# Order of ScalarE's weight parts in the seven-product MLPs, and where the conditioning slabs of block three are loaded

## The reference, cut to what matters

```
def squared_relu_mlp(h, w_in, w_out):                 # width 4096, twice, in block one
    return jnp.square(jax.nn.relu(h @ w_in)) @ w_out
def swiglu(h, w_gate, w_up, w_down):                  # width 2816, twice, in block two
    return (jax.nn.silu(h @ w_gate) * (h @ w_up)) @ w_down
def swiglu_ffn(h, w_ffn_in, w_ffn_out):               # width 2816, once, in block three
    gate, up = jnp.split(h @ w_ffn_in, 2, axis=-1)
    return (jax.nn.silu(gate) * up) @ w_ffn_out
mod = jax.nn.silu(c) @ w_ada + b_ada                  # c: 1024 values, w_ada: 1024 x 6144
```

## Time and profile before

| | |
|---|---|
| median of 3 runs | 3456.21 us (3449.58 to 3465.32) |
| the profiled execution's own time | 3448.42 us |
| its span, first to last instruction | 3446.5 us |
| mean granted TensorE clock | 0.992 |
| busy: PE, PEld | 3295.1 us (96%), 2701.5 us (78%) |
| busy: DVE, POOL, ACT | 2036.9 us (59%), 1803.1 us (52%), 1105.2 us (32%) |
| read from HBM | 308.15 MB |
| chain that ended last | PE 76%, DVE 11%, POOL 5%, ACT 4%, DMA 2% |

### The profile page before, as it was taken

How to read it: one execution, slowest core, us unless ns; L and a number is a source line. 1 busy time by engine, 2 the same in 40 slices (tenths; PEclk the granted TensorE clock), 3 DMA queues, 4 the chain that set the end, 5 groups by cost and what they waited for, 6 DMA issues and landing times.

```text
span 3446.5 us, 51330 instructions
## 1 busy us (share of the span) xinstructions
PE 3295.1 (96%) x21318; PEld 2701.5 (78%) x21318; DVE 2036.9 (59%) x3132; ACT 1105.2 (32%) x2317; POOL 1803.1 (52%) x1387
## 2 busy tenths in 40 slices
PE   8999999999978989999999988999999999999998
PEld 6768788986767778888878778778887776778996
DVE  6554444458476567688662475564436657657665
ACT  2241101357443344344402432110002225224443
POOL 7526566641234457455666001666665735745563
PEclk9999999999999999999999999999999999999999
DMA  5203434320123333233333101423323635513231
GB/s 178 77 29 106 134 100 145 100 68 26 38 86 110 110 110 116 86 113 109 116 98 110 38 2 43 143 92 98 97 87 126 221 92 176 171 44 104 93 114 52
DMA packets 262152, 341.08 MB, mean 99 GB/s; under 512 B 10016, under 2 KB 202784, under 8 KB 259360
## 3 DMA queue, kind: packets, MB, share of 16 engines
q1 hardware_dynamic: 239408, 301.51, 27.3%
q10 hardware_dynamic: 22512, 36.28, 3.0%
HBM read 308.15 MB, written 25.43 MB: 97 GB/s over the span
## 4 chain that ended last, share of the span: by engine, by line
PE 76%; DVE 11%; POOL 5%; ACT 4%; DMA 2%; issue 1%; ACTq 0%; DVEq 0%; SPq 0%; POOLq 0%
PE bank L130 74%; POOL wlo L153 3%; DVE wlo L153 2%; PE bank L133 2%; ACT whi L148 1%; DVE hl L153 1%; DVE scr L153 1%; POOL sq L153 1%; DMA raw<-in_ffn_w_gate 1%; ACT gt L148 1%; POOL whi L160 1%; DVE macc L163 0%; DVE st L168 0%; DMA raw<-in_w_mlp_in 0%; ACT ah L148 0%
## 5 line engine op out<-in xcount | busy, mean ns | idle before, releaser
L153 POOL TENSOR_TENSOR wlo<-raw,whi 128x512 fp32r<-128x512 f32 x762 | 1060.5, 1422 | 474.0 <-ACT whi L148 460.9
L130 PE MATMUL bank<-ah,whi 128*128 128x512 f32 (+1 forms) x2408 | 869.3, 361 | 33.7 <-ACT scr L148 9.3
L160 POOL TENSOR_SCALAR whi<-raw 128x1024 fp32r<-128x1024 f32 x313 | 364.2, 1182 | 1015.9 <-PE bank L130 506.7
L130 PE MATMUL bank<-ah,wlo 128*128 128x512 f32 (+1 forms) x2408 | 859.9, 357 | 0.0
L130 PE MATMUL bank<-al,whi 128*128 128x512 f32 (+1 forms) x2408 | 848.3, 357 | 0.9 <-DVE al L163 0.9
L130 PEld LDWEIGHTS bank<-ah,whi 128*128 128x128 f32 x2408 | 452.8, 188 | 125.2 <-ACT scr L148 10.1
L130 PEld LDWEIGHTS bank<-al,whi 128*128 128x128 f32 x2408 | 452.8, 188 | 77.2 <-DVE al L163 1.8
L130 PEld LDWEIGHTS bank<-ah,wlo 128*128 128x128 f32 x2408 | 453.1, 188 | 73.5 <-issue 0.2
L130 PE MATMUL bank<-hh,whi 128*128 128x512 f32 x1040 | 417.2, 401 | 23.4 <-DVE hl L153 23.4
L130 PE MATMUL bank<-hl,whi 128*128 128x512 f32 x1040 | 414.0, 398 | 0.0
L130 PE MATMUL bank<-hh,wlo 128*128 128x512 f32 x1040 | 413.1, 397 | 0.0
(11 more groups left out here) (484 smaller groups left out, 5394.2 us busy)
## 6 DMA issues: line engine op xcount, KB each, us to landing
raw<-in_w_in SPq DMA_DIRECT2D x34, 1024.0 KB, 5.3
raw<-in_w_mlp_in SPq DMA_DIRECT2D x32, 1024.0 KB, 5.5
raw<-in_w_mlp_out SPq DMA_DIRECT2D x32, 1024.0 KB, 5.2
raw<-in_w_ada SPq DMA_DIRECT2D x24, 1024.0 KB, 5.2
raw<-in_ffn_w_gate SPq DMA_DIRECT2D x22, 1024.0 KB, 5.5
raw<-in_ffn_w_up SPq DMA_DIRECT2D x22, 1024.0 KB, 5.3
raw<-in_w_ffn_in SPq DMA_DIRECT2D x22, 1024.0 KB, 5.1
raw<-in_w_out SPq DMA_DIRECT2D x16, 1024.0 KB, 5.2
```

What stands on the lines that cost most here:

```text
L130: return self.eng.matmul(out, lhsT, rhs, start=start, stop=stop, skip_group_check=True)
L153: return IDLE if self.eng is None else self.eng.tensor_tensor(out, a, b, op)
L160: return self.eng.tensor_scalar(out, a, s1, s2, op0, op1)
```

## The change

It does two things. In each step of a seven-product MLP ScalarE makes the high parts of the down tiles before it copies P1, not after. And the number of conditioning calls becomes a count that each MLP is given: mlp0 makes one call behind each `first(g)` and two behind each `second(g-1)` (8 + 14 = 22 calls), mlp1 one in each step as before (14, calls 22 to 35), and ffn1 none. The calls in mlp0 take 15 slabs and 7 sets of matmuls (10 and 5 before), those in mlp1 take 9 slabs and 5 sets (10 and 4 before).

```diff
@@ mlp_pe
             if g:
                 second(g - 1)
-                if ada and g < len(groups):
+                for _ in range(ada if g < len(groups) else 0):
                     self.ada_pe(e)
@@ paired_act
+            self.outs_high_act(a, o)
             some(parts, 1)
-            self.outs_high_act(a, o)
             some(high, not opens)
@@ mlp_dve
-                if ada and not end:
+                for _ in range(0 if end else ada):
                     self.ada_dve(d)
@@ relu_mlp_pe
-        self.mlp_pe(e, name, None, (self.A["w_mlp_in"][l], 0), self.A["w_mlp_out"][l], 32, self.mlp1_t[l], True,
+        self.mlp_pe(e, name, None, (self.A["w_mlp_in"][l], 0), self.A["w_mlp_out"][l], 32, self.mlp1_t[l], 2 - l,
@@ relu_mlp_dve
-        self.mlp_dve(d, name, False, 32, self.mlp1_t[l], add, True, True, True, nxt, amid=amid)
+        self.mlp_dve(d, name, False, 32, self.mlp1_t[l], add, True, True, 2 - l, nxt, amid=amid)
@@ ffn2_pe
-                    22, self.mlp1_t[0], name == "ffn1", self.roots_once(e, f"n{name}", prev, False),
+                    22, self.mlp1_t[0], 0, self.roots_once(e, f"n{name}", prev, False),
@@ ffn2_dve
-        self.mlp_dve(d, name, True, 22, self.mlp1_t[0], add, True, name == "ffn1", name == "ffn1", nxt,
+        self.mlp_dve(d, name, True, 22, self.mlp1_t[0], add, True, name == "ffn1", 0, nxt,
@@ ffn3_pe and ffn3_dve: False becomes 0
```

More of the change, by code:

```diff
@@ L4086, in ffn3_pe @@
         W = self.A["w_ffn_in_3"][0]
-        self.mlp_pe(e, "ffn3", (W, 0), (W, 2816), self.A["w_ffn_out_3"][0], 22, self.mlp1_t[0], False,
+        self.mlp_pe(e, "ffn3", (W, 0), (W, 2816), self.A["w_ffn_out_3"][0], 22, self.mlp1_t[0], 0,
                     opening=lambda parts: self.opening_pe(e, self.ln1, parts), last=self.ln2)
@@ L4100, in ffn3_dve @@
         add = lambda d, n, bank, out: d.stt(out, bank[:, :], self.mod(5, n), self.x[:, n, :], MUL, ADD)
-        self.mlp_dve(d, "ffn3", True, 22, self.mlp1_t[0], add, False, False, False, None)
+        self.mlp_dve(d, "ffn3", True, 22, self.mlp1_t[0], add, False, False, 0, None)
         self.ln2_dve(d)
```

## The result

The changed kernel takes 3403.99 us (median of 4 runs, 3400.13 to 3407.53), beside 3454.68 us for the kernel before (4 runs, 3449.58 to 3465.32). The ratio is 0.9849, with a 95% interval of 0.9823 to 0.9875: 50.7 us faster, about 1.5%. The forecast was 3398. The profiled execution took 3404.76 us; the sum for it was 3393, so in the terms 11.8 us are missing; most of them can be found one by one.

What follows compares the result with a forecast made beforehand. TensorE, busy 3295.1 of 3446.5 us, bounds the kernel, so only its holes can be gained. Terms -31.6 - 7.1 - 7.1 - 20.7 + 11 = -55.5 us give 3393, adjusted to 3398 us; 8-in-10 range 3378 to 3428.

Steps and rivals of the forecast that it cites:

- -33.4 in twelve steps: mlp1: of 37.0 us of stalls in twelve steps, 3.6 stay once the down tiles' high parts come first.
- The stalls left: mlp1: 0.3 us of stall remains in each step, bounds 0 and 1.2.
- The fifth call of the third kind: mlp1: one more conditioning call of the sort costing TensorE 1.79 us, with narrow matmuls and a wait for x: +1.8 us.
- The landing that was foreseen as the next late thing: mlp1: the next pair's slab lands 5.0 us into the step; its loop of 20.8 us just fits TensorE's 21.0.
- -7.1 each for the order: ffn1 and ffn3: high parts first save 3.6 us in fifteen steps and 3.5 in the four-out step, each.
- the wide step's 4.1: ffn3's first step with four outs takes 25.14 us, 4.1 over its matmuls; 3.5 of that was to go.
- the missing conditioning: ffn1: without conditioning slabs, pair slabs no longer land late and its rotation becomes ffn3's: -20.7 us, bounds -10 and -22.
- the mis-sized term: mlp0: five more slabs and two more matmul sets cost +11 us, from queued loads and waits; bounds +2 and +35.
- Rival 1: mlp1: VectorE, slowed beside GpSimd, becomes the bound at 23.4 us a step; only 15.6 of 33.4 come: 3416 us, chance 0.16.
- Rival 2: mlp0 pays at every half group because GpSimd never gets ahead: +35 in place of +11, 3422 us, chance 0.12.
- Rival 3: No change: the landing alone sets P5 in mlp1, and mlp0 takes what ffn1 gives: about 3450 us, chance 0.07.
- Rival 4: Slower: the down slab has not landed when ScalarE asks for it, so P1 is late: 3530 us, chance 0.05.

Runs made afterwards that it cites:

- Experiment 2: The changed kernel with ScalarE's old order, so the moved conditioning calls alone: 3457.54 us, ratio 1.0008 to the kernel before.
- experiment 1: The kernel before with only ScalarE's down-tile high parts put ahead of P1, conditioning calls unmoved: 3403.55 us, ratio 0.9859.
- experiment 3: The changed kernel with mlp0's conditioning slab load placed between the next half group's two weight slabs, not ahead of both: 3386.6 us.
- experiment 5: The 3386.6 us kernel (experiment 3) with mlp1's macc ahead of the hidden low parts and mods behind the next step's additions: 3375.15 us.
- experiment 4: The kernel before with the down tiles' high parts moved still later, behind P5: 3598.8 us, ratio 1.0421.

## Why the prediction was right, and where its sizes were off

**The total.** 3398 stands nearer to 3403.99 than the terms deserve, by luck. The terms were 11.8 us short for the profiled execution. The 4.9 us added at the end, mostly for the median standing 7.8 over that execution, hid part of this; in the changed kernel the median stands 0.8 under the profiled execution.

**mlp1.** Forecast -33.4 in twelve steps, measured 296.24 - 264.04 = -32.2. The stalls left were taken as 0.3 us a step; they are (264.04 - 252.0 - 7.2) / 12 = 0.4. The fifth call of the third kind: forecast +1.8, the end of mlp1 measured +2.0. The signs came as named: steps of 21.1 to 22.1 (forecast 21.3) and 22.8 (forecast 23) us, waits for ScalarE's `gt` of 0 (under 5). The landing that was foreseen as the next late thing does hold P5 up in the step shown, where the high part waits 1.31 us for it and P5 is done at 6.6 and not at 5.2; but it is in time, and only four of the twelve steps have such a wait (5.1 us in all).

**ffn3 and ffn1.** Forecast -7.1 each for the order. ffn3: -3.4 and -4.1, together -7.5, though 1.4 were lost between ffn3's start and these steps. Of the wide step's 4.1 I had left 0.6 standing; it went down to the matmuls. Part of it had been clock: 0.93 in the earlier trace rows, 1.00 after. In ffn1 the order and the missing conditioning together gave 24.1 and 4.2 us, forecast 27.8. Experiment 2 has the conditioning at 20.0 (forecast 20.7), so the term was right in size. That the holes were the loads is in part argued: experiment 2 takes away the loads and VectorE's conditioning work at once (its busy time falls from 198.83 to 174.13 us). What speaks for the loads are ScalarE's waits for a landing just ahead of such holes (4.41 us in the earlier trace rows, 6.24 in experiment 1), and that VectorE is busier than before in the changed kernel's ffn1 (206.23 us) while TensorE has no hole there.

**mlp0, the mis-sized term.** Forecast +11, measured +17.7 in it and +1.1 up to mlp1. The waits were forecast well: 8 us, a larger one at every second group border; the trace has 8.9 in four (2.4, 2.3, 2.1 and 2.1, at every second border) and 0.8 in one, less the 0.6 of before, and two sets make 1.6. The other 7.0 us are in no wait. Most of them are in the matmuls behind each wait:

```profile
424.70 0.47 PE L130 MATMUL bank<-ah,whi 128*128 128x512 f32 x1 [2.26 <-POOL wlo L153]
...
425.95 0.63 PE L130 MATMUL bank<-al,whi 128*128 128x512 f32 x1
426.38 0.63 PE L130 MATMUL bank<-ah,wlo 128*128 128x512 f32 x1
...
428.89 0.39 PE L130 MATMUL bank<-ah,wlo 128*128 128x512 f32 x1
429.12 0.40 PE L130 MATMUL bank<-ah,whi 128*128 128x512 f32 x1
```

Their pitch is 0.43 us, not 0.233, for about 3.5 us. The sums of that stretch, and of the one behind the first late group's wait:

```profile
424.70:428.94 4.24, 4.24 (x12) 3.34 (x13) 3.23 (x3) 0.00 (x0) 4.16 (x3) 0.60 0.02 4
...
329.24:333.20 3.96, 3.96 (x11) 3.10 (x12) 3.22 (x3) 0.00 (x0) 3.88 (x3) 0.58 0.02 4
```

Granted clock 0.60 and 0.58: most of it at the 1.2 GHz level, after TensorE had done nothing but narrow matmuls and waiting for 3.2 and 3.4 us. Twelve matmuls at 0.233 would take 2.8 us and took 4.24. Over the first forty matmuls behind each of the four waits it is 10.96 us against 9.42 for the same ones in experiment 3, which has no wait there: each wait costs 1.5 us more than its row in the list of waits says, 6.1 us in all. The two sets took 0.95 us each and not 0.8, and the last 0.6 us I did not place. TensorE: Matmul & The Clock Gate of the Trainium skill ("Part 1: The HAM clock gate") has a gate that grants half or all of the clock by how busy the engine has lately been; the pitch of 0.43 us here agrees. The forecast priced stalls by their length alone: in the earlier trace rows the one stall of mlp0 before was 0.62 us, with no such tail, and that is why I took none. But the trace of the kernel before did hold the tail for a wait of the forecast length. It is the 0.93 of the wide step in the earlier trace rows:

```profile
3377.44 0.36 PE L130 MATMUL bank<-h,whi 128*128 128x256 f32 x1 [2.35 <-ACT gt L148]
```

Behind this wait, with no narrow matmuls ahead of it, the granted clock is 0.60 from 3377.30 to 3381.60.

**The rivals.** Rival 1 (VectorE the bound in mlp1) did not come as a whole, but a piece of it is there: in the steps of 22.1 us TensorE waited 0.85 us for VectorE's `gt`, and experiment 5 took that away. VectorE and GpSimd in such a step of the changed kernel:

```profile
1078.70 5.11 DVE L163 SCALAR_TENSOR_TENSOR macc<-raw,mc,macc 128x512 f32<-128x512 f32 x4
```

```profile
1078.68 1.30 POOL L153 TENSOR_TENSOR wlo<-raw,whi 128x512 fp32r<-128x512 f32 x1 [1.85 <-ACT whi L148]
1081.06 1.42 POOL L153 TENSOR_TENSOR wlo<-raw,whi 128x512 fp32r<-128x512 f32 x1 [1.07 <-ACT whi L148]
```

`macc` is 2.0 us longer than the 3.11 of the earlier trace rows, with 2.7 us of GpSimd's low parts in its time. The rule of the Trainium skill cited in the prediction (SBUF — State Buffer, "SBUF: two separate sides"), that one excludes the other, would make it 2.7: near, and in that direction. In experiment 5 it is farther off: 5.6 us of GpSimd's sums lie in the 6.33 us of the four instructions, which are 3.2 us longer and not 5.6. But the wait that came of it is 0.85 us in four of twelve steps, where the rival left each step 2.4 us over the 21.0. Rival 2 (every half group pays) did not come: four of them paid. Rival 3 (no change) did not come, as the order by itself gave 51 us (experiment 1); its other half, that mlp0 takes what ffn1 gives, is what experiment 2 shows. Rival 4 did not come: in mlp1 and ffn1 ScalarE has no wait for a down slab.

**Where the rest of the 11.8 us lies.** mlp0 and the way behind it were 7.8 dearer than forecast; mlp1 as a whole 1.4; ffn1 and ffn3 gave 0.8 more; 3.4 are spread over mixers and openings, among them 1.2 ahead of mlp0 and the 1.4 at ffn3's start. What these last are I did not try to find.

## What to carry to other kernels

Where engines run in a fixed order, put work whose inputs are long there ahead of the first wait on the bottleneck, and price the move along the longest chain that hangs on it: here the four pieces of 2.18 us held 5.5 us of GpSimd, and experiment 4 shows that stages which seemed to have slack can pay too. A load that has to wait for a late buffer belongs behind the loads that are needed next, not ahead of them. And a wait of TensorE is to be priced with the slower matmuls behind it, where the trace has such a tail behind waits of its length.

## What the runs showed of the hardware that I had not expected

A wait of 2.3 us with narrow matmuls ahead of it was followed by 4.2 us at a granted clock of 0.60, and so was one of 2.35 us without them in the kernel before, while the waits of 0.85 us in the changed kernel's mlp1 were followed by no such fall. Between the two the traces give no sharp line: of the fifteen waits of up to 1.9 us in the twelve steps of the kernel before, two were followed by 3.41 us at a granted clock of 0.50 (from 1186.81 and 1285.80). In experiment 4 one wait of 4.9 to 6.2 us in each step brought the mean granted clock of twelve steps to 0.89. And a kernel that did the same work with VectorE busier and GpSimd busier (experiment 3 against the changed kernel, in mlp0) was 17 us faster: the same instructions of both took longer in sum, and this cost nothing where TensorE did not wait for either.
